# Splitting the first weight chunks and spreading early modulation chunks in a two-block fp32 transformer kernel

## The reference, cut

```
h  = rms_norm(x, norm_mix_pre)              # block 1
z  = h @ w_in                               # zq zf zb zi zg zu zv ga gb
b_out = gelu(zu) * (spatial mix of layer_norm(gelu(zv)))
a_out = hgrn2(silu(zq), gates(zf), gates(zb), zi) * silu(zg)
...                                         # merge, w_out, SwiGLU hidden layer, per-layer embedding
mod = silu(c) @ w_ada[i] + b_ada[i]         # block 2, used from there on only
h  = rmsnorm(x) * (1 + scale) + shift       # Fourier mixer, SwiGLU, retention, SwiGLU, final norm
```

## Time and profile before

| | |
|---|---|
| median of 3 runs | 1172.46 us (1171.18 to 1173.0) |
| profiled execution | 1173.02 us |
| its span in the trace | 1170.1 us |
| mean granted PE clock | 0.994 |
| busy: PE, DVE, ACT | 98%, 71%, 46% of the span |

### The profile page before, as it was taken

One profiled execution on the slowest core, in us unless ns is written; L12 is line 12 of the kernel. 1 busy time (PEld: TensorE's weight loads), 2 busy tenths in 40 slices (PEclk: granted clock), 3 DMA queues, 4 the chain that ended last, 5 costly groups with the idle time before them and its releaser, 6 DMA issues.

```text
span 1170.1 us, 14019 instructions
## 1 busy us (share of the span) xinstructions
PE 1145.0 (98%) x5840; PEld 966.8 (83%) x5840; DVE 835.0 (71%) x957; ACT 539.3 (46%) x521; POOL 27.5 (2%) x51
## 2 busy tenths in 40 slices
PE   6999999999999999999999999999999999999997
PEld 5998898888788888888788888879976887888886
DVE  4789987987666767567656767478955866767655
ACT  5566656643544444456463434344422435434432
POOL 1000000000000000000000000000001000000000
PEclk8999999999999999999999999999999999999999
DMA  7763463438447778542447687458753564786761
GB/s 289 298 227 144 167 265 135 154 144 304 169 176 293 268 274 315 214 145 96 159 178 294 257 309 290 189 186 318 289 199 123 204 263 144 258 304 260 295 247 38
DMA packets 38638, 259.81 MB, mean 222 GB/s; under 512 B 4144, under 2 KB 6448, under 8 KB 7856
## 3 DMA queue, kind: packets, MB, share of 16 engines
q1 hardware_dynamic: 36960, 251.84, 58.1%
q0 software_dynamic: 1616, 7.08, 1.7%
HBM read 257.86 MB, written 1.05 MB: 221 GB/s over the span
## 4 chain that ended last, share of the span: by engine, by line
PE 83%; DVE 9%; DMA 3%; issue 2%; ACT 2%; POOL 1%; SPq 0%; POOLq 0%; ACTq 0%; DVEq 0%
PE pair L428 42%; PE pair L493 20%; PE pair L454 7%; PE pair L509 4%; DVE w_lo L1196 4%; PE tp L550 3%; PE tp L612 2%; DMA raw<-stream 2%; DMA mskf<-masks 1%; PE tp L785 1%; PE pair L724 1%; PE tp L713 1%; ACT w_hi L816 1%; PE tp L639 1%; PE tp L763 1%
## 5 line engine op out<-in xcount | busy, mean ns | idle before, releaser
L1196 DVE TENSOR_TENSOR w_lo<-raw,w_hi 128x2048 fp32r<-128x2048 f32 x182 | 413.3, 2287 | 91.6 <-ACT w_hi L816 91.0
L816 ACT ACTIVATE w_hi<-raw 128x2048 fp32r<-128x2048 f32 x182 | 347.4, 1915 | 226.3 <-DMA raw<-stream 143.0
L428 PE MATMUL pair<-w_hi,ht_lo 128*128 128x512 f32 x816 | 326.5, 400 | 14.1 <-DVE w_lo L1196 14.1
L428 PE MATMUL pair<-w_lo,ht_hi 128*128 128x512 f32 x816 | 319.2, 391 | 0.0
L428 PE MATMUL pair<-w_hi,ht_hi 128*128 128x512 f32 x816 | 318.9, 391 | 0.0
L428 PEld LDWEIGHTS pair<-w_hi,ht_lo 128*128 128x128 f32 x816 | 154.0, 189 | 47.8 <-DVE w_lo L1196 16.0
L428 PEld LDWEIGHTS pair<-w_lo,ht_hi 128*128 128x128 f32 x816 | 153.8, 188 | 32.9
L428 PEld LDWEIGHTS pair<-w_hi,ht_hi 128*128 128x128 f32 x816 | 154.2, 189 | 31.4 <-issue 1.2
L1205 DVE SCALAR_TENSOR_TENSOR raw<-raw,crow 128x1024 f32<-128x1024 f32 x112 | 132.3, 1218 | 0.8 <-DMA raw<-stream 0.8
L493 PE MATMUL pair<-w_hi,gt_lo 128*128 128x512 f32 x272 | 107.3, 395 | 0.3 <-DVE gt_lo L1268 0.3
L493 PE MATMUL pair<-w_lo,gt_hi 128*128 128x512 f32 x272 | 106.0, 390 | 0.0
(11 more groups left out here) (221 smaller groups left out, 1251.5 us busy)
## 6 DMA issues: line engine op xcount, KB each, us to landing
raw<-stream SPq DMA_DIRECT2D x238, 1024.0 KB, 4.9
xres<-x SPq DMA_DIRECT2D x2, 512.0 KB, 6.7
prow<-rows POOLq DMA_DIRECT2D x1, 1024.0 KB, 10.3
xres<-x POOLq DMA_DIRECT2D x2, 512.0 KB, 4.8
dt<-decay POOLq DMA_DIRECT2D x1, 1024.0 KB, 6.9
outT<-outb SPq DMA_DIRECT2D x4, 256.0 KB, 2.3
csr<-dft POOLq DMA_DIRECT2D x1, 768.0 KB, 4.3
crow<-rows POOLq DMA_DIRECT2D x1, 512.0 KB, 6.7
```

The lines of the kernel that those rows point to most:

```text
L428: mm = pe.matmul(pair[use % 2][:, t, :], a[:, 4 * c + k, t * P:(t + 1) * P], b[:, w % WS, k * 512:(k + 1) * 512], start=(c == 0 and k == 0 ...
L816: sc.activation(w_hi[:, w % WS, :], raw[:, n % RAW, :], ACT.Copy).then_inc(hi_done, 1)
L1196: v.tensor_tensor(w_lo[:, w % WS, :], raw[:, n % RAW, :], whi32[:, w % WS, :], ALU.subtract).then_inc(raw_done, 1)
```

## The change

The first two weight chunks are handled in four pieces of 512 columns each: chunk 0 is also loaded in four pieces (`first_in`), chunk 1 in one. The semaphores `hi_done` and `raw_done` therefore count four for each of the first two chunks (`pieces_done`). Stage zu runs chunk by chunk over both token tiles (`first_part`), each inner step waiting for its piece; the four half tiles are turned in between, and eight more warm-up products stand behind the first. zv then runs as an ordinary `wide` stage. The loads of x tile 1 and the columns change places with what stood before them, and crow's load, its silu, the wait for it, hgrow and the mask conversion move later. Modulation chunks leave ticks 0, 1, 2, 5, 17 and the last of down2, and are placed at 6, 8, 37 and at step j = 1 of each hidden layer. In `head_gates` on DVE, tick(W0[b]) moves ahead of the backward keys.

```diff
+ADA_FIRST = 1
-    return [W0[name] + 2 * j - 1 for j in range(FIRST, GROUPS)]
-ADA_TICKS = [0, 1, 2, 5, 17, 18, 20, 31, 33]
+    return [W0[name] + 2 * j - 1 for j in range(ADA_FIRST, GROUPS)]
+ADA_TICKS = [6, 8, 18, 20, 31, 33, 37]
-ADA_TICKS += ffn_adas("ffn2") + [W0["down2"] + j for j in (2, 4, 6)]
+ADA_TICKS += ffn_adas("ffn2") + [W0["down2"] + j for j in (2, 4)]
+LATE_ADA = W0["wa"] + 3
...
+PIECES = 4
+FINE = 2
+def pieces_done(n):
+    return n + 1 + (PIECES - 1) * min(n + 1, FINE)
...
             sp.dma_start(xres[:, 0, :], x[:, 0, :]).then_inc(x_in[0], 16)
             sp.dma_start(idn[:], ident).then_inc(small_in, 16)
+            sp.dma_start(xres[:, 1, :], x[:, 1, :]).then_inc(x_in[1], 16)
             sp.dma_start(col[:], cols).then_inc(small_in, 16)
-            sp.dma_start(raw[:, 0, :], stream[0]).then_inc(landed[0], 16)
-            sp.dma_start(xres[:, 1, :], x[:, 1, :]).then_inc(x_in[1], 16)
+            for q in range(PIECES):
+                sp.dma_start(raw[:, 0, q * 512:(q + 1) * 512], stream[0][:, q * 512:(q + 1) * 512]).then_inc(first_in[q], 16)
...
-            pool.dma_start(crow[:], rows[4:5, :].to_broadcast([P, D])).then_inc(crow_in, 16)
             rsqrt(RQ["norm0"], 2)
-            pool.wait_ge(hi_done, 2)
+            pool.wait_ge(hi_done, pieces_done(2))
             pool.dma_start(sgw[:], sg_wT).then_inc(sgu_in, 16)
...
+            pool.wait_ge(hi_done, pieces_done(5))
+            pool.dma_start(crow[:], rows[4:5, :].to_broadcast([P, D])).then_inc(crow_in, 16)
             pool.dma_start(hgrow[:].rearrange("p a b -> p (a b)"), rows[1:2, :].to_broadcast([P, D])).then_inc(hg_in, 16)
...
+            def first_part(c, t, after={}):
+                n = SPLIT[tile_job("norm0", t, c)] + 1
+                for k in range(4):
+                    piece = PIECES * c + k + 1
+                    if t == 0:
+                        pe.wait_ge(hi_done, piece)
+                    if k == 0:
+                        pe.wait_ge(t_hi, n)
+                    out = pair[USE["zu"] % 2][:, t, :]
+                    ki, tk, wk = 4 * c + k, slice(t * P, (t + 1) * P), slice(k * 512, (k + 1) * 512)
+                    pe.matmul(out, ht[0][:, ki, tk], w_hi[:, c, wk], start=(c == 0 and k == 0), stop=False)
+                    if t == 0:
+                        pe.wait_ge(raw_done, piece)
+                    pe.matmul(out, ht[0][:, ki, tk], w_lo[:, c, wk], start=False, stop=False)
+                    if k == 0:
+                        pe.wait_ge(lo_done, n)
+                    mm = pe.matmul(out, ht[1][:, ki, tk], w_hi[:, c, wk], start=False, stop=(c == 1 and k == 3))
+                    if k in after:
+                        after[k]()
...
+            def next_halves():
+                first_tile(1, 0, xn_half, 2)
+                first_tile(0, 1, xn_done, 1)
...
-            turn_tile("norm0", xn, 0, xn_done, 1)()
-            turned_head(W0["zu"], USE["zu"], turn_tile("norm0", xn, 1, xn_done, 2), "norm0")
+            first_tile(0, 0, xn_half, 1)
+            keep_warm(8)
+            first_part(0, 0, after={0: next_halves})
+            first_part(0, 1, after={1: lambda: first_tile(1, 1, xn_done, 2)})
+            first_part(1, 0)
+            first_part(1, 1)
+            wide(W0["zv"], USE["zv"])
...
             norm_squares(RQ["norm0"], 0, 0)
-            split_hi(0)
-            norm_his("norm0", 0, colv("mix_pre", 0, 8))
-            split_hi(1)
             norm_squares(RQ["norm0"] + 1, 1, 0)
+            for q in range(2):
+                hi_piece(0, q)
+            norm_hi("norm0", 0, 0)
+            for q in range(2, PIECES):
+                hi_piece(0, q)
+            first_scaled(0)
+            norm_hi("norm0", 1, 0)
+            for q in range(PIECES):
+                hi_piece(1, q)
+            norm_hi("norm0", 0, 1)
+            first_scaled(1)
+            norm_hi("norm0", 1, 1)
             for w in range(2, WS):
                 split_hi(w)
-            act.wait_ge(crow_in, 16)
-            sc.activation(crow[:], crow[:], ACT.Silu).then_inc(ca_done, 1)
-            norm_his("norm0", 1, colv("mix_pre", 0, 8))
...
                 sc.activation(qf[:], pair[USE[q] % 2][:].rearrange(as4, b=2), ACT.Silu).then_inc(evac[USE[q] % 2], 1)
+                if half == 0:
+                    act.wait_ge(crow_in, 16)
+                    sc.activation(crow[:], crow[:], ACT.Silu).then_inc(ca_done, 1)
...
-                    if j >= FIRST:
+                    if j >= ADA_FIRST:
                         ada(ADA_AT[w + 2 * j - 1])
...
                 read_banks()
+                tick(W0[b])
                 link(keys(1, b, kb))
...
                 v.tensor_tensor(qf[:], qf[:], tf[:], ALU.mult).then_inc(hg_qupd, 1)
-                tick(W0[b])
                 tick(W0[b] + 1)
...
-            norm(RQ["norm0"], 0)
+            mean_square(RQ["norm0"])
+            first_norm(0, 0, xn_half)
+            first_norm(0, 1, xn_done)
             dve.wait_ge(small_in, 32)
-            norm_jobs("norm0", 0, colv("mix_pre", 0, 8))
-            split_lo(0)
-            split_lo(1)
-            norm(RQ["norm0"] + 1, 1)
+            mean(RQ["norm0"] + 1)
+            first_scaled(0)
+            dve.wait_ge(rstd_done, RQ["norm0"] + 2)
+            first_norm(1, 0, xn_half)
+            lo_piece(0, 0)
+            norm_lo("norm0", 0, 0)
+            for q in range(1, PIECES):
+                lo_piece(0, q)
+            first_norm(1, 1, xn_done)
+            norm_lo("norm0", 1, 0)
+            first_scaled(1)
+            lo_piece(1, 0)
+            norm_lo("norm0", 0, 1)
+            for q in range(1, PIECES):
+                lo_piece(1, q)
+            norm_lo("norm0", 1, 1)
             split_lo(2)
             split_lo(3)
-            norm_jobs("norm0", 1, colv("mix_pre", 0, 8))
...
             tick(W0["wa"] + 3)
             turned_tile("tm", ht, ht32, 1)
+            ada(ADA_AT[LATE_ADA])
```

93 lines of the change are left out of this document (64 added, 29 removed).

## The result

The changed kernel takes **1162.33 us** (median of 4 runs, 1161.54 to 1163.92) against 1172.22 us for the kernel before in the same comparison: a ratio of 0.9914, 95% interval 0.9903 to 0.9926, so 0.74% to 0.97% faster. The forecast was 1163.2 us, from 1160.8 to 1168.5.

The account below looks back on a forecast made before the run. It took PE, busy 98% of the span, as the bound, gaining only where idle, slow-clocked or given less work. 5.8 + 2.6 - 0.5 + 0.3 + 1.4 = 9.6 us off 1173.0 gave 1163.4, stated as 1163.2, range 1160.8 to 1168.5.

Parts of the forecast that it names:

- The signs that the prediction named: First product about 12, clock 1.00 from 1 to 30 us, feature chunk about 35, no masked-copy waits, among others.
- rival (a): First stage: late columns or quarters and waits for parts pace PE; gain only 6.1, time 1167; chance 0.18.
- The start, 5.8 predicted: First zu product: starts at 11.8 instead of 17.60, a gain of 5.8 us, bounds 4.3 and 6.2.
- The fixed time of about 2 us for a transfer: Quarter loads of chunk 0: if paid one after another, products fed some 2 us later, sum 1165; landings showed no such addition.
- I keep 8.2: Columns' landing, when PE starts turning: kept at 8.2 with x tile 1 ahead and crow gone; bounds 7.8 and 9.7.
- The clock, 2.6 predicted: First stage, up to the first feature chunk: full clock makes it 22.9 us instead of 25.5, a gain of 2.6.
- rival (b): Thin beginning of the first stage: the clock falls once more, the 2.6 us is not won, time 1166.0; chance 0.08.
- Start and clock and transposes: Up to the first feature chunk: gains 5.8 and 2.6, less 0.5 for twelve transposes instead of eight behind the start.
- Waits behind the start, 0.3 + 1.4 predicted: Chunks 4 to 7 and the masked copies: 0.3 us from modulations leaving the start, 1.4 from moving tick(W0[b]).
- The modulations taken out of the start: Ticks 0, 1, 2, 5: freeing DVE of 9.4 us removes a late split's wait, a gain of 0.3 us.
- tick(W0[b]), 1.4 predicted: head_gates: the masked copy comes 2.2 us earlier, more than either wait, key gates not later; gain 1.4 us.
- Modulations moved later, nothing predicted: Tick 37 and hidden layers' j=1: fit into idle DVE time, chunk 48 keeps 3.5 us to spare; no cost.

Follow-up runs that it names:

- e5: Changed kernel with chunk 0 loaded as one 1 MB transfer instead of four, the work still split in four pieces; 1165.78 us, ratio 0.9936.
- e9: Changed kernel with crow's 0.5 MB load put back at the start of POOL's list; 1165.06 us, ratio 0.994.
- e1: Kernel before with the new start alone; modulations, crow and tick(W0[b]) stay in their old places; 1168.96 us, ratio 0.9962.
- e3: Kernel before with 30 unneeded products between the turning of tile 0 and the first real product; 1173.02 us, ratio 1.0005.
- e11: Kernel before with only tick(W0[b]) moved ahead of the key gates; 1172.8 us, ratio 0.9996.
- e2: Kernel before with everything of the change but the start: modulations, crow and tick(W0[b]) as in the changed kernel; 1168.11 us, ratio 0.9954.
- e10: Changed kernel with seven products filling the wait at ffn0's head, and the columns loaded second, before identity and x tile 1; 1164.19 us, ratio 0.9917.
- e4: Changed kernel without the eight warm-up calls behind the first turning; 1164.66 us, ratio 0.9936.
- e7: Changed kernel with 32 instead of 8 warm-up calls before the first product; 1166.65 us, ratio 0.9942.
- e6: Changed kernel with tick(W0[b]) moved back behind the copies in head_gates; 1171.89 us, ratio 0.9998.
- e8: Changed kernel with seven unneeded products in PE's wait at the head of the first hidden layer; 1161.73 us, ratio 0.9912.

## Why the prediction was right, and where its terms were off

The signs that the prediction named came: first product at 11.29, feature chunk at 34.94, no wait for the masked copy, no new wait on w_lo between 35 and 100 us or in a hidden layer. PE had no wait for a piece between 11.29 and 34.94, so rival (a) did not come. The parts of the sum did less well than the sum.

**The start, 5.8 predicted, 6.3 measured.** The chain was the predicted one: quarter, two pieces, ht_hi, product. The columns came 0.4 later than assumed (8.56), and the warm-up ended at 11.00 instead of 11.8, because its sixteen passes took 1.95 us and not 3.0. That price was the mean of the first 36 passes, most of which run in the first 6 us at about half the pace. The last link was ACT. The quarters carry it: without them e5 is 1.85 us later here and 3.2 at the feature chunk. The fixed time of about 2 us for a transfer (the Trainium skill, DMA: Bandwidth & Descriptors, section Anatomy of one DMA, fitted there on transfers that GpSimd issues, while the quarters are SP's) was left out of the sum. The four quarters took 7.0 us at the median from issue to landing, and ACT had the first at 9.37, earlier than the whole chunk landed before (10.50). If that fixed time is paid, it is not paid by one transfer after the other.

**"I keep 8.2": this step was right only in its result.** It let x tile 1 ahead of the columns and crow's leaving cancel. e9 measures crow alone: 2.4 us at the feature chunk, 1.1 of it by the clock (e1 has 1.2 in all). With crow beside them the columns took 6.5 to 8.2 us in the five kernels that load it at the start (before, e1, e3, e9, e11), and 3.5 to 6.7 in the eight that don't. The term should have been split in two: x tile 1 ahead of the columns costs them something like 0.6 to 2.7 us (4.0 in e2, 4.6 to 6.7 in the six kernels with x tile 1 ahead and without crow), and crow's absence gives about that back. The spread of those six, whose loads up to the columns are the same, says how little one profile fixes such a number. e10 shows that nothing is to be had from undoing the first, since x tile 1 is then late.

**The clock, 2.6 predicted, and the first stage.** Start and clock and transposes were to give 7.9 at the feature chunk and gave 8.2. The granted clock was 1.00 in every window from 8 to 36 us, so rival (b) did not come. e3, at full clock, reaches the feature chunk 2.0 us earlier, after a first product 0.2 later, so the clock was worth 2.2 us there. e4 shows that the rival was near: 2.81 us without work and the clock was 0.50 at the first products. What the eight warm-up calls buy is 0.9 us at the feature chunk. On the transposes (the Trainium skill, TensorE: Matmul & The Clock Gate, section Part 4: PE-mode transpose) these runs don't decide: in the changed kernel the clock stood at 1.00 with eight transposes at 12.49, but products stood on both sides of them.

**Waits behind the start, 0.3 + 1.4 predicted, 2.8 measured.** The places were right: chunk 7, and the two copies. The lead grew by 0.7 to the end of chunk 9, by 1.15 more at the first levels and by 0.95 at the second half, where the list of waits had 0.3, 0.91 and 0.5. The list counts idle time only; the lead shows what each wait costs with what follows it (behind the wait of 0.91 the eight score products took 1.16 us, the eight before it 1.05).

**The modulations taken out of the start: the mechanism was right, and it is worth more than its 0.3.** The prediction counted the wait that there was. e3 and e1 show what there would have been: with PE early and the modulations in place, 1.8 and 2.8 us of the lead are lost up to the end of chunk 9. Of the new start's 7.0 us only 4.7 reached the end in e1. Spreading DVE's work and loads is what lets the lead through, and e7 shows it passing one for one up to 300 us. How much of this is the modulations and how much the masks and crow is not shown: no kernel moved the modulations alone.

**tick(W0[b]), 1.4 predicted: this is the step of the sum that failed.** It priced the move as DVE time in front of the masked copy, 2.2 us against waits of 0.91 and 0.5. In the kernel before that move brings 0.4 us in the profile (0.7 less what was there ahead of it) and nothing that the times can tell (e11): at the first half one wait takes the place of the other, since the split delays the keys. That the key gates are not later held in the changed kernel (75.24, when ACT has kb) and not in that one (86.25 instead of 84.58). In the changed kernel its absence costs 9.8 us by the ratios, and 7.3 of it are a single wait (e6), which ends with the staging copies and not with the masked copy. The expectation for e6, made with the same reasoning, named some 3.7 us; the copy accounts for about 3.2 of the loss, and the rest was not foreseen. What was missing is a loop through four engines: a late split frees its raw buffer late, the load into it lands late, ACT stands in order at that chunk's w_hi with the staging copies behind it, and PE's scores wait for those. The prediction looked at who waits for DVE, and not at who waits for the buffer that DVE frees.

That e11 gains nothing and e6 loses everything is no contradiction. With three buffers each load goes where the chunk three places ahead in the stream was. With a modulation at tick 8, chunk 14's load takes chunk 12's buffer, which is this tick's split; without one it takes chunk 11's. The rows agree: in e6 SP issued it at 84.19, after chunk 12's split (84.16), in the kernel before at 83.50, after chunk 11's (83.47). e1 has the late tick and an early PE but no modulation at tick 8, and there ACT did not wait for chunk 14 to land; its two waits for the copy came to 0.9 us. So the modulation that the change put at tick 8 is what makes the tick's place matter. An early PE does not seem to be needed, because the keys follow PE (they start 2.2 us behind the end of chunk 9 in e6, 2.6 in the kernel before); no kernel with the old start, the late tick and a modulation at tick 8 was run.

**Modulations moved later, nothing predicted.** Chunk 48 was priced to have 3.5 us to spare. Its split ended at 330.5 and PE asked at 333.4: 2.9. There is no new wait at any hidden layer's j = 1 to 3. DVE's hole before the norm in front of the first hidden layer was still 2.93 us long with the extra modulation in it.

**What came unforeseen** is the 2.7 us given back. The 1.4 of the clock at the first hidden layer look like chance and not like the change: all eleven profiles with that wait open have it at 2.27 to 2.31 us, and the clock fell in four (the changed kernel, e2, e4, e9) and not in seven, the kernel before among these. The four executions of the changed kernel differ in the same way: a mean granted clock of 0.996 goes with 1163.92 us, 0.997 with 1163.02, and 0.998 with 1161.63 and 1161.54. Only the first of them has a profile, so the place of the others' loss is not shown. Without the fall the profiled execution would have taken about 1162.5 us. The closeness of the sum (1163.4) to the profiled 1163.9, and of forecast to median (0.9 us), owes something to luck, by errors that cancel: 11.0 won and not 9.6 (0.3 more up to the feature chunk, 1.1 behind it), then 2.7 given back.

**Still open**: the stores. Their median landing is 2.3 us in the four kernels with the old start (before, e2, e3, e11) and 2.5 to 2.9 in those with the new one, 1150 us later. It isn't the number of SP's transfers: e5, with one load in place of four, has 2.6. The late wait at 946 also wasn't tried by itself; it is in the changed kernel's and e4's profiles and in no other.

## What to carry to other kernels

Work moved out of a start is worth what it lets through, not the waits it was seen to cause: find the engine that is second in line there, and check that an earlier first engine isn't simply caught by it. Where loads run through a ring of buffers, price a moved step by the buffer it frees too, and count again whose buffer each load takes when a load is moved: follow that buffer's next load to the engine that takes it in order, and to everything that stands behind it. A broadcast load that nobody needs yet can hold up a small load that everybody needs.

## What the runs showed of the hardware

- A wait of 2.3 us without work lets TensorE's clock fall in some executions and not in others (four of eleven, at 302 us), at a cost of 1.4 us. With seven products put into the wait it stayed at 1.00 in both kernels that had them (e8, e10), and e8's four runs lie within 0.45 us. Two profiles don't prove it, as seven of eleven kept the clock without them.
- After a wait of 0.88 us sixteen passes took 1.95 us; after one of 2.36 us they took 3.04 (granted clock 0.54, e9), and after one of 2.03 us 1.95 again (e1).
- In or soon behind waits of 1.7 us (e1, at 55.30), 1.8 us (e5, at 13.14) and 7.3 us (e6, at 93.03) the granted clock went down to about 0.5; after one of 2.1 us (e3, at 60.63) it stayed at 1.00. The length of the wait alone does not tell in these rows.
- Four transfers of 256 KB in place of one of 1 MB brought the first data to ACT 2.0 us sooner (9.37 against 11.33) and PE had no new wait for a load behind them.
- A 512 KB broadcast on GpSimd's queue beside them took the 100 KB of columns on SP's queue from 6.4 to 8.2 us, and the quarters from 7.0 to 8.4 (one profile each; without it the columns took 4.6 to 6.7 over six kernels).
- A 1 MB load issued when no other was on its way took 4.7 us from issue to landing (e6, at 84.19).
